# A two-block sequence model on one Trainium2 core: the attention pairs of the second block's front, with four probability buffers, scaling on ScalarE and the selections spread between the pairs

## The reference, cut to what matters

```python
score = einsum('bqhs,bqh->bqs', relu(einsum('bqhd,bsd->bqhs', qib, k_idx)), wib) * idx_scale
score = where(causal, score, -inf)
_, sel = top_k(score, topk)                       # topk = 128
logits = einsum('bqhd,bqkhd->bqhk', qb, kg) * Dh ** -0.5
prob = softmax(where(valid, logits, -inf))
out = einsum('bqhk,bqkhd->bqhd', prob, vg)
```

## Time and profile before

| | |
|---|---|
| median of 3 runs | 2718.43 us (2717.89 to 2723.14) |
| the profiled execution's own time | 2719.01 us |
| its span, first to last instruction | 2717.3 us |
| mean granted TensorE clock | 0.961 |
| PE busy | 2547.8 us (94%) |
| DVE busy | 1039.9 us (38%) |
| ACT busy | 558.3 us (21%) |
| POOL busy | 1498.4 us (55%) |

### The profile page before, as it was taken

How to read it: one execution, slowest core, us unless ns; L and a number is a source line. 1 busy time by engine, 2 the same in 40 slices (tenths; PEclk the granted TensorE clock), 3 DMA queues, 4 the chain that set the end, 5 groups by cost and what they waited for, 6 DMA issues and landing times.

```text
span 2717.3 us, 34707 instructions
## 1 busy us (share of the span) xinstructions
PE 2547.8 (94%) x14410; PEld 2061.8 (76%) x14410; DVE 1039.9 (38%) x1667; ACT 558.3 (21%) x1127; POOL 1498.4 (55%) x1396
## 2 busy tenths in 40 slices
PE   7998997999999998999999989868589998999998
PEld 6778886888888886568888878645488687888887
DVE  3443857163051401336404164973542151421023
ACT  1112323021020113741102021224332210210010
POOL 7444554587496664337749636621121565666664
PEclk9997998999999998999999998989798999999999
DMA  5222022233232231003324313210000222333321
GB/s 165 78 56 63 1 86 85 78 115 95 70 123 94 80 107 62 1 32 105 98 69 124 93 45 90 64 53 16 1 3 2 74 86 85 93 98 97 93 79 69
DMA packets 104289, 199.06 MB, mean 73 GB/s; under 512 B 9306, under 2 KB 12612, under 8 KB 104132
## 3 DMA queue, kind: packets, MB, share of 16 engines
q1 hardware_dynamic: 101476, 189.36, 22.8%
q10 hardware_dynamic: 2656, 7.47, 0.8%
HBM read 194.71 MB, written 2.10 MB: 72 GB/s over the span
## 4 chain that ended last, share of the span: by engine, by line
PE 84%; DVE 10%; ACT 2%; POOL 2%; issue 1%; SPq 0%; DMA 0%; DVEq 0%; POOLq 0%; ACTq 0%
PE psum L153 34%; PE psum L293 23%; PE psum L155 7%; PE psum L232 3%; PE psum L1260 1%; PE psum L1251 1%; PE psum L1279 1%; POOL weight_split_ring L412 1%; DVE big L1810 1%; PE psum L2090 1%; PE psum L2099 1%; DVE best L1809 1%; PE psum L968 1%; PE psum L2075 1%; PE psum L194 1%
## 5 line engine op out<-in xcount | busy, mean ns | idle before, releaser
L412 POOL TENSOR_TENSOR weight_split_ring<-weight_ring,weight_split_ring 128x512 fp32r<-128x512 f32 (+2 forms) x732 | 955.6, 1326 | 30.6
L153 PE MATMUL psum<-x_split,weight_split_ring 128*128 128x512 f32 x4080 | 963.1, 396 | 1.9 <-POOL weight_split_ring L412 1.3
L153 PEld LDWEIGHTS psum<-x_split,weight_split_ring 128*128 128x128 f32 x4080 | 770.2, 190 | 173.3 <-issue 11.8
L409 POOL TENSOR_SCALAR weight_split_ring<-weight_ring 128x1024 fp32r<-128x1024 f32 (+2 forms) x366 | 395.6, 1081 | 759.0 <-PE psum L293 339.9
L293 PE MATMUL psum<-weight_split_ring,hidden_split 128*128 128x512 f32 x2448 | 576.5, 396 | 8.2 <-DVEq L2899 8.2
L293 PEld LDWEIGHTS psum<-weight_split_ring,hidden_split 128*128 128x128 f32 x2448 | 460.3, 188 | 120.0 <-DVEq L2899 8.6
L155 PE MATMUL psum<-weight_split_ring,x_split 128*128 128x512 f32 (+2 forms) x1056 | 238.0, 385 | 2.0 <-DVEq L2899 1.4
L155 PEld LDWEIGHTS psum<-weight_split_ring,x_split 128*128 128x128 f32 x1056 | 195.2, 205 | 43.7 <-issue 7.2
L708 DVE TENSOR_TENSOR big<-big 128x512 f32<-128x512 f32 x64 | 89.0, 1391 | 178.4 <-ACT big L693 178.4
L511 DVE SCALAR_TENSOR_TENSOR residual<-residual,psum 128x512 f32<-128x512 f32 x48 | 32.8, 682 | 261.9 <-PE psum L293 261.9
L693 ACT ACTIVATE big<-psum 128x512 f32<-128x512 f32 x64 | 38.3, 599 | 434.9 <-PE psum L153 378.8
(11 more groups left out here) (329 smaller groups left out, 2627.6 us busy)
## 6 DMA issues: line engine op xcount, KB each, us to landing
weight_ring<-in_mlp_w SPq DMA_DIRECT2D x128, 512.0 KB, 3.8
weight_ring<-in_w_in SPq DMA_DIRECT2D x92, 512.0 KB, 3.6
weight_ring<-in_w_ffn_in SPq DMA_DIRECT2D x40, 512.0 KB, 3.6
weight_ring<-in_w_out SPq DMA_DIRECT2D x24, 512.0 KB, 3.7
weight_ring<-in_w_ffn_out SPq DMA_DIRECT2D x22, 512.0 KB, 3.6
weight_ring<-in_sb_w_q SPq DMA_DIRECT2D x8, 512.0 KB, 3.6
weight_ring<-in_sb_w_k SPq DMA_DIRECT2D x8, 512.0 KB, 3.8
weight_ring<-in_sb_w_v SPq DMA_DIRECT2D x8, 512.0 KB, 3.7
```

The costliest lines, as they stand in the source:

```text
L153: mm = pe.matmul(out, wp[:, k, m * P:(m + 1) * P], xp, start=first, stop=last)
L409: pool.tensor_scalar(part.high[:, 0:nk, 0:n], raw, 1.0, 0.0, ALU.mult, ALU.add).then_inc(self.high_made, 1)
L412: low = pool.tensor_tensor(part.low[:, k, 0:n], raw[:, k, :], part.high[:, k, 0:n].bitcast(F32), ALU.subtract)
```

## The change

Four things change, all in the pair loop of `second_front`.

1. `m.prob` has four buffers (index i % 4) in another place of the same memory, and `exp(i)` waits for the transposes of head i-4.
2. ScalarE's order in a turn becomes `exp(2p)`, `exp(2p+1)`, `copy(2p-2)`, the two scalings of pair p, `copy(2p-1)`. The scaling is an activation Copy with the inverse row sum as its scale, in place; VectorE keeps only the reciprocal (`inverse(p)`), which it now issues at the end of its turn.
3. VectorE's order in a turn becomes both `peak`, the selection rounds, `shift`, `inverse(p)`.
4. `choose(2)` is spread over turns 0 to 6 with 2, 2, 2, 2, 3, 3, 2 rounds, and `choose(3)` over turns 7 to 11 with 3, 3, 3, 3, 4.

```diff
+    CHOICE = [2, 2, 2, 2, 3, 3, 2, 3, 3, 3, 3, 4]
...
-                mm = pe.transpose(kit.psum[:, 6, block(b)], m.prob[:, i % 2, block(b)], m.ident[:, :])
+                mm = pe.transpose(kit.psum[:, 6, block(b)], m.prob[:, i % 4, block(b)], m.ident[:, :])
...
-            if i >= 2:
-
-                act.wait_ge(s_pt, i - 1)
-            act.activation(m.prob[:, i % 2, 0:n], kit.psum[:, 4 + i % 2, 0:n], ACT.Exp, bias=m.nmax[:, i % 4, :],
+            if i >= 4:
+
+                act.wait_ge(s_pt, i - 3)
+            act.activation(m.prob[:, i % 4, 0:n], kit.psum[:, 4 + i % 2, 0:n], ACT.Exp, bias=m.nmax[:, i % 4, :],
...
+        def normalise(p):
+            n = pair(p)[2]
+            act.wait_ge(s_inv, p + 1)
+            for s in range(2):
+                x = m.prob[:, (2 * p + s) % 4, 0:n]
+                act.activation(x, x, ACT.Copy, scale=m.prec[:, s, :]).then_inc(s_sc, 1)
...
             if p < PAIRS:
                 exp(2 * p)
+                exp(2 * p + 1)
             if 1 <= p <= PAIRS:
                 copy(2 * p - 2)
             if p < PAIRS:
-                exp(2 * p + 1)
+                normalise(p)
             if 1 <= p <= PAIRS:
                 copy(2 * p - 1)
...
-        choose(2)
         shift(0)
         shift(1)
         for p in range(PAIRS + 2):
-            if 1 <= p <= PAIRS:
-                normalise(p - 1)
-            for n in landed(p - 1):
-                shift(n)
-            if p < NHEAD:
-                choose(3, p, NHEAD)
             if p < PAIRS:
                 peak(2 * p)
                 peak(2 * p + 1)
+            if p < 7:
+                choose(2, CHOICE[p], p == 0, p == 6)
+            elif p < 12:
+                choose(3, CHOICE[p], p == 7, p == 11)
+            for n in landed(p - 1):
+                shift(n)
+            if p < PAIRS:
+                inverse(p)
...
-        self.prob, self.probT = self.part(b, 9984, 2, SEQ), self.part(b, 7168, 2, SEQ)
+        self.prob, self.probT = self.part(b, 4096, 4, SEQ), self.part(b, 7168, 2, SEQ)
```

More of the change, by code:

```diff
@@ L1440, in second_front @@
     s_p = kit.sem("exponentials_ready")
+    s_inv = kit.sem("row_inverse_ready")
     s_sc = kit.sem("probabilities_ready")
@@ L1795, in add_term, with choose @@
                 dve.scalar_tensor_tensor(out=sc, in0=r, scalar=w, in1=sc, op0=ALU.mult, op1=ALU.add).then_inc(s_acc, 1)
-        def choose(t, part=0, parts=1):
+        def choose(t, rounds=ROUNDS, first=True, last=True):
             sc, wk = score(t), m.work[:, 0:(t + 1) * P]
-            if part == 0:
+            if first:
                 dve.wait_ge(s_fut, t + 1)
@@ L1805, in choose @@
             else:
-                if part == 0:
+                if first:
                     step(dve.tensor_scalar(wk, sc, IDX_SCALE, None, ALU.mult))
-                for _ in range(ROUNDS // parts):
+                for _ in range(rounds):
                     step(dve.max(m.best[:, :], wk))
                     step(dve.match_replace(wk, m.best[:, :], wk, REMOVED))
-                if part < parts - 1:
+                if not last:
                     return
@@ L1830, in peak, with inverse @@
                .then_inc(s_max, 1)
-        def normalise(p):
-            n = pair(p)[2]
+        def inverse(p):
             dve.wait_ge(s_p, 2 * p + 2)
             rows = slice((2 * p) % 4, (2 * p) % 4 + 2)
[L1836 to L1839, removed]
+            dve.reciprocal(m.prec[:, :, 0], m.psum_row[:, rows, 0]).then_inc(s_inv, 1)
         mu0 = m.col0["mu"]
@@ L1853, in vector @@
             elif i >= 2 * NHEAD:
-                choose(1, i - 2 * NHEAD, 2 * NHEAD)
+                choose(1, 1, i == 2 * NHEAD, i == STEPS - 1)
         for t in range(NT):
```

## The result

The changed kernel takes 2690.88 us (median of 4 runs, 2689.02 to 2692.61), the kernel before 2718.16 us beside it. The ratio is 0.9898, 95% interval 0.988 to 0.9917: 27 us less, where 26 to 27 less was forecast (2692 us, range 2686 to 2704).

The account below looks back on a forecast made before the run. A ring of waits between engines, not a shortage, bounds the 137.5 us pair loop. New loop: 90.8 floor + 15.6 waits + 1.6 GpSimd + 2.5 clock = 110.5 us, 27 less: 2692 us, range 2686 to 2704.

Parts of the forecast that it names:

- The entry wait: At the loop's start TensorE stands still 17.21 us for pair 0's exponentials; part 4 was to remove it wholly.
- The ring: Two buffers tie exponentials to the previous pair's end; parts 1 and 2 remove 11.1 us of waits and most copy waits.
- TensorE's floor of 90.8 us: TensorE's work alone in the pair loop, same matmuls before and after: 84.8 us plus four wide steps.
- Waits in its place, 15.6 us: New TensorE waits in the loop: 3.8 us in turns 0 to 6, 9.3 in 7 to 11, 2.5 in 12 to 17.
- ScalarE's scaling: 512-wide scaling on ScalarE: 0.58 us start to start, 0.69 duration, no table load; loop 1.5 us less to 5.9 more.
- The clock: The fall in the 17 us wait goes; turns 7 to 12 may have one: 0 to 6 us, 2.5 taken.
- The clock before: In the old loop, 6.8 us of 1776.7 to 1801.1 ran at 1.2 GHz, costing up to 3.4 us.
- Its own range: 2686 to 2698 us: low without clock fall or GpSimd, high with 3.2, 6 and 4 us of slower scaling.
- The signs: Waits before `out` largest in turns 8, 9, 11 to 13; wrong if pairs 2 to 6 exceed 5.5 us.
- Rival 1: Chain from peak to `out` longer, through slower scaling and rounds or clock falls: 2704 us, 2698 to 2710; chance 0.23.
- Rival 2: No gain: the 17 us returns where a bias is needed, before `logits(8)` or `logits(12)`; 2718 us, chance 0.05.
- Rival 3: Slower: TensorE stays at 1.2 GHz through the loop because of small waits every turn; about 2766 us, chance 0.04.

Follow-up runs that it names:

- rest_alone: Changed kernel with part 4 undone: choose(2) whole ahead of the loop, choose(3) in two rounds in each of turns 0 to 7; 2698.23 us.
- spread_alone: Kernel before with part 4 alone, selections spread over turns 0 to 11, all else as before; 2723.95 us, ratio 1.0018.
- buffers_alone: Kernel before with only the four buffers and both exponentials ahead of the copies on ScalarE; 2705.30 us, ratio 0.9955.
- early_and_inverse: Changed kernel with seven choose(2) rounds ahead of the first shifts, the others redistributed, and the reciprocal after one round of each turn; 2676.36 us.
- vector_scales: Changed kernel with the two scalings of a pair back on VectorE, behind the reciprocal; 2685.49 us, ratio 0.9886.
- double_scaling: Changed kernel with one more copy of the same size ahead of each scaling on ScalarE, into unread memory; 2697.91 us.
- seven_early_vector: Changed kernel with seven choose(2) rounds ahead of the first shifts, the others redistributed, and scalings on VectorE; 2687.98 us.

## Why the prediction was right, point by point

- **The entry wait goes.** Right for the whole change: the second logits start after 3.62 us, some 3.7 forecast. Right too that part 4 takes it: without part 4, rest_alone keeps 12.7 us of it, and with part 4 alone 1.9 is left. Wrong to book it as a gain, "the 17.2 us goes wholly": spread_alone loses, and part 4 on top of the rest brings 5.8 us. The parts aren't terms of a sum. What is a sum is the floor and the waits that an order leaves.
- **The ring goes.** Right: no wait for an exponential, and buffers_alone takes away the 14 later ones.
- **TensorE's floor of 90.8 us.** Too low by 2.9: the same matmuls take 93.7 us with the clock at its upper level throughout (early_and_inverse). The term at fault is the second transpose group of a turn, taken at 0.35 us like the first, which a wide step follows. Ahead of the logits it takes 0.53 (1846.59 - 1846.06 in the changed kernel), 0.18 more, which is 2.9 us in 16 pairs:

```profile
1846.06 0.60 PE L1560 MATMUL psum<-constants,big 128*128 128x128 f32 x4
1846.59 1.13 PE L1546 MATMUL psum<-big 64*128 64x512 f32 x4
```
- **Waits in its place, 15.6 us.** 10.8 + 3.5 = 14.3 measured, and the 1.6 us taken for GpSimd are in this. Ahead of `out` 13.8 was worked out (bias 1.8 left aside), so 3 too many; for the bias 3.5 instead of 1.8, since two closing instructions took 1.63 and 1.37 us beside GpSimd:

```profile
1821.88 1.63 DVE L1825 SCALAR_TENSOR_TENSOR big<-big 128x512 f32<-128x512 f32 x1
1823.55 1.37 DVE L1826 TENSOR_SCALAR hidden_split<-big 128x512 fp32r<-128x512 f32 x1
...
1824.98 1.16 PE L1552 MATMUL psum<-hidden_split,exact_identity 128*128 128x512 f32 x2 [3.46 <-DVE hidden_split L1826]
```

In vector_scales they took 0.69 and 0.43 us. GpSimd was at its two subtractions from 1821.43 to 1824.64. The 1.6 us that was taken for GpSimd is 1.9 here.
- **ScalarE's scaling.** 0.71 us at 512, 0.61 from start to start, against 0.69 and 0.58:

```profile
L1693 ACT ACTIVATE big<-big,prob_inverse 128x512 f32<-128x512 f32 x8 | 5.3, 712 | 0.0
1851.96 1.32 ACT L1693 ACTIVATE big<-big,prob_inverse 128x512 f32<-128x512 f32 x2
```

The Trainium skill's advice (ScalarE: Activation LUTs, Rules for kernel authors) to keep a multiplication on VectorE is not contradicted: vector_scales is no slower. No scaling carries a table load. Its price is as small as was forecast, while twice the time costs 7 us.
- **The clock.** One fall, 6.8 us at 1.2 GHz behind a wait of 3.46 us and a late chain; it cost some 3.2 us (busy 96.9 against 93.7), 2.5 was taken. Six waits of 0.8 to 2.2 us ahead of `out` in the first 71 us brought none.
- **The clock before.** The prediction reads 6.8 us at the lower level, all from the fall in the long wait. The trace has more: that fall ends before 1782, a second stands near 1788 to 1794 (0.53 from 1791 to 1794) and a third near 1814 to 1821 (0.50 from 1816 to 1819). Together they cost 8.3 us of busy time, not 3.4. So the old order carried forward, 133.6 us, did not leave out just 4 us of clock and GpSimd: it holds 42.8 us of waits (133.6 - 90.8), and the trace has 35.2.
- **The sum.** Loop 111.2 us against 110.5, but not by the terms as they stand. Measured it is 93.7 of work, 3.2 for the clock and 14.3 of waits; forecast it was 90.8, 2.5 and 17.2 (15.6 and 1.6). The floor is 2.9 too low and the waits 2.9 too high, so that the number comes within 0.7 us is in part luck. The mechanism, long waits and the ring replaced by shorter waits ahead of `out`, is what the rows show.
- **Its own range.** 90.8 + 15.6 + 3.2 + 6 + 4 = 119.6 us, which is 2701 us and not 2698. The range as a whole doesn't change.
- **The signs.** Waits ahead of `out` are largest in turns 8, 9 and 11 (2.16, 1.60 and 1.40 us), as forecast. Pairs 13 and 14 take 6.38 and 6.61 us, 6.2 to 6.5 forecast. Two of the signs of being wrong did appear, each in part: of pairs 2 to 6, which were not to take over 5.5 us, pair 5 took 6.16 (the others 4.4 to 5.2), and the clock stood at 0.5 for 6.8 us, more than the 6 that were named. Pair 5's wait is 1.25 us, in the second row below, and the price of the clock the 3.2 above.

```profile
1774.85 0.70 PE L1546 MATMUL psum<-big 64*128 64x256 f32 x4
...
1777.24 0.44 PE L1571 MATMUL psum<-big 128*64 128x128 f32 x4 [1.25 <-ACT big L1698]
...
1781.01 0.70 PE L1546 MATMUL psum<-big 64*128 64x256 f32 x4
```

**The rivals.** Rival 1 (a longer chain): double_scaling made it so, +7 us, so the mechanism is real and its size was not reached. Rival 2: no; a bias was waited for, 3.5 us of it. Rival 3: no, 0.97 granted over the loop. Nor had TensorE stayed at the lower clock in the kernel before, as it says: the earlier trace rows has 0.86 over the 24.4 us behind the long wait.

## What to carry to other kernels

When an order is written by hand, work out the fixed work of the engine that bounds (each piece with what follows it: 0.35 and 0.53 us for the same transposes), then carry all queues forward turn by turn in the new order; a wait in the old trace is not the gain of the edit that names it, as spread_alone shows with a loss. Within a turn, put what others wait for (peaks, then the reciprocal) ahead of work that only has a due date (the selection rounds), and put such work into idle time ahead of the loop. Two edits that attack different causes, the length of a queue and the place in it, came near to adding up in the loop: 6.0 and 7.0 us alone, 11.4 together. By the medians they did less so: 9.1 and 11.7, 14.5 together.

## What the runs showed that was not expected

- VectorE's closing instruction with two tensor inputs took 1.63 us when GpSimd was busy and 0.69 when not, in the same code in two orders. Small reorderings can therefore move the time by a microsecond or more that no count of instructions tells.
- The phases around an edit moved by 3 us each way between single executions (the loop began at 1749.99 to 1755.9 in the profiles of kernels with the same code ahead of it). Whether the loop's own length is steadier is not shown, since each kernel has one profile. It was always above what the queues carried forward gave: by 3 to 6 us in nine of the thirteen kernels, and by 8 to 13 us in buffers_alone, double_scaling (6 us added to the changed kernel's 106.6), seven_early_vector and spread_alone. Of each, 2.9 us is the floor. The lower clock, which was not carried forward, is another 4.6, 7.4, 4.1 and 16.1 us in the last four, in that order; what then remains, up to 6 us either way, is in the waits and was not taken apart.
